# The state-space part of a two-layer block: steps of four tokens, two rounds in place of eight, and GpSimd's products moved to VectorE

## The chip, the cores and the metric

The kernel runs on one core of one Trainium2 chip. The metric is the device time of one execution in microseconds (us), from the core's first instruction to its last; it is reported as the median of several runs. The engines are named TensorE (PE, its weight loads PEld), VectorE (DVE), ScalarE (ACT), GpSimd (POOL) and SyncE (SP).

## The reference

`x` is 256 tokens by 1024 channels, float32. A first block of two layers (feed-forward, mixer, feed-forward; the mixers are attention with a gated linear recurrence, and a gated convolution) is followed by a second block of two layers, each a "mix2" mixer and a feed-forward part, the last one a mixture of 8 experts. Each mix2 mixer splits its input into a state-space group (S5, 512 channels) and a gated linear attention (GLA). Of the S5 group, cut to what matters (32 groups of 16 channels, 64 complex states each):

```python
lam_bar = jnp.exp(lam * dt)
b_bar = ((lam_bar - 1.0) / lam)[:, :, None] * b_mat
bu = jnp.einsum('gph,blgh->blgp', b_bar, u_c.astype(jnp.complex64))
a_cum, s = lax.associative_scan(_linear_recurrence_op, (a_elems, bu), axis=1)
states = s + a_cum * h[:, None]
y = jnp.einsum('ghp,blgp->blgh', c_mat, states).real
...
y = y.transpose(1, 0, 2, 3, 4).reshape(bsz, seq, S5_WIDTH) + d_skip.astype(f32) * uf
y = jax.nn.gelu(y).astype(u.dtype)
return y * jax.nn.sigmoid(y @ w_glu + b_glu)
```

The recurrence is s[t] = lam_bar * s[t-1] + bu[t], one complex number for each state.

## The kernel before

The program is a list of ten parts (`SUBS`, numbered b): 0 to 5 are the first block, 6 is mix2, 7 a feed-forward part, 8 mix2, 9 the experts. The second block's layer is n = (b - 6) // 2, so mix2 runs twice. A part eats "units" of weights: SyncE loads a unit (1 MB `raw_gu`, 0.5 MB `raw_d`) into one of two raw buffers, ScalarE rounds it (`hi`, into `wh_gu`, `wh_d`), VectorE takes the rest (`lo`, into `wl_gu`, `wl_d`), and TensorE multiplies in three terms (`mm3`). Each engine runs its own list in the order of the code; semaphores (`wait_ge`, `then_inc`) bind them, and `link` is a wait of an engine for its own last result.

In a feed-forward part (b = 5 and b = 7 here) TensorE does for each unit r the products of `gate_up(r)` (48 matmuls of 256 columns) and then `down(r-1)` (12 of 512 columns).

In mix2, TensorE first streams units U to U+5 (q, k, alpha, v, output gate `go`, and the S5 inputs u), and puts the eight level products of GLA (`level(j)`, L2047 and L2066) behind blocks of that stream; VectorE prepares each level (`differences`, `decayed`, `masked`), ScalarE does the exponentials (`decay`). Then comes the S5 stage. The states are turned by powers of the phase of lam_bar, so that the recurrence has a real factor and VectorE's scan instruction can do it: `table(n)` on GpSimd computes these powers `E` for all 256 tokens in feed-forward parts 5 and 7. Then eight rounds r follow, of two state tiles each: TensorE `bu(r)` (L2130), VectorE `turn_in(r)` (L1319 to L1322), a sum and a difference (L1339, L1340), four scans of 256 tokens (L1344), `turn_back(r)` (L1329, L1330), GpSimd two more products (L1705, L1706), TensorE the output products (L2154). `gated_heads` and `mixed_heads` of GLA lie in rounds 0 and 1; `skip(t)` adds the direct term. After them come gelu, XH and XL (L710, L1361), and TensorE's GLU unit, whose first matmul waits for `yl`. B and C of each round or layer come by DMAs that GpSimd issues.

## Time and profile before

| what | value |
|---|---|
| median of 3 runs | 2754.56 us (2746.49 to 2756.39) |
| span of the profiled execution | 2747.2 us |
| PE busy | 2600.3 us, 95% of the span |
| PEld busy | 2379.0 us, 87% |
| DVE busy | 2165.5 us, 79% |
| ACT busy | 1483.6 us, 54% |
| POOL busy | 947.8 us, 34% |
| mean granted TensorE clock | 0.971 |
| DMA | 670.58 MB, 244 GB/s on the mean |

The profile gives the profiled execution's own time as its span, 2747.2 us, which lies between the lowest and the highest of the three runs. Busy time is the sum of an engine's instructions; of TensorE it says how long it had matmuls in it, not that it ran at its peak. The granted clock is 1.0 at 2.4 GHz and 0.5 at 1.2 GHz. Times in the rows below are microseconds from the span's start; the first mix2 runs from about 1067 to 1243, the second from about 1497 to 1673.

### The profile page before, as it was taken

What the parts mean: (1) busy time and instruction counts of PE and PEld (TensorE: products, weight loads), DVE (VectorE), ACT (ScalarE), POOL (GpSimd) and SP (SyncE); (2) the same over time, 40 slices, a digit from 0 to 9 for tenths busy, and PEclk for the clock granted to TensorE, in tenths of its full rate; (3) what the DMA queues carried; (4) which work ended last, traced back from release to release, by engine and by line L of the source; (5) the groups of instructions that cost most, each with busy time, mean ns of one, the idle gap of its engine ahead of it and who ended that gap; (6) DMA issues with size and microseconds to landing.
All of it is one profiled execution on the core that took longest, in us unless ns stands there. A gap on an engine that the chain in (4) does not pass through costs nothing. (4 is left out here: it accounts for less than half of the span.)

```text
span 2747.2 us, 47482 instructions
## 1 busy us (share of the span) xinstructions
PE 2600.3 (95%) x17802; PEld 2379.0 (87%) x17802; DVE 2165.5 (79%) x2488; ACT 1483.6 (54%) x1930; POOL 947.8 (34%) x586
## 2 busy tenths in 40 slices
PE   8999899999998998888998978999999999999997
PEld 7999699999897998658998747999999999999986
DVE  5667666766787676987855997898989898989888
ACT  4337543443434334424334515777777777777765
POOL 6990089688789992126900130000000000000000
PEclk9999999999999998999999988999999999999999
DMA  8664267566566653324553415999999999999985
GB/s 309 252 237 148 103 241 256 202 250 254 191 241 229 220 183 134 115 105 164 183 184 138 164 63 192 343 350 333 352 335 349 338 347 343 347 345 346 340 320 216
DMA packets 129209, 670.58 MB, mean 244 GB/s; under 512 B 14672, under 2 KB 14992, under 8 KB 80064
## 3 DMA queue, kind: packets, MB, share of 16 engines
q1 hardware_dynamic: 111024, 604.72, 59.9%
q0 software_dynamic: 18064, 64.21, 6.9%
q8 instruction: 81, 1.33, 0.2%
q14 instruction: 40, 0.33, 0.0%
HBM read 667.82 MB, written 1.05 MB: 243 GB/s over the span
## 5 line engine op out<-in xcount | busy, mean ns | idle before, releaser
L1721 PE MATMUL work<-xT_hi,wh_gu 128*128 128x256 f32 x2088 | 593.9, 284 | 21.6 <-DVE xT_lo L985 12.0
L1722 PE MATMUL work<-xT_lo,wh_gu 128*128 128x256 f32 x2088 | 592.3, 284 | 0.0
L1723 PE MATMUL work<-xT_hi,wl_gu 128*128 128x256 f32 x2088 | 591.7, 283 | 0.0
L1721 PE MATMUL work<-wh_gu,mixT_hi 128*128 128x256 f32 x1792 | 507.5, 283 | 2.8 <-DVE wl_gu L1439 1.5
L1722 PE MATMUL work<-wl_gu,mixT_hi 128*128 128x256 f32 x1792 | 505.8, 282 | 0.0
L1723 PE MATMUL work<-wh_gu,mixT_lo 128*128 128x256 f32 x1792 | 505.5, 282 | 0.0
L857 DVE TENSOR_TENSOR wl_gu<-raw_gu,wh_gu 128x2048 fp32r<-128x2048 f32 x158 | 392.3, 2483 | 72.0 <-ACT wh_gu L395 71.5
L1721 PEld LDWEIGHTS work<-xT_hi,wh_gu 128*128 128x128 f32 x2088 | 401.3, 192 | 30.1 <-issue 21.3
L1722 PEld LDWEIGHTS work<-xT_lo,wh_gu 128*128 128x128 f32 x2088 | 401.7, 192 | 4.8
L1723 PEld LDWEIGHTS work<-xT_hi,wl_gu 128*128 128x128 f32 x2088 | 401.5, 192 | 0.0
L862 DVE TENSOR_TENSOR wl_d<-raw_d,wh_d 128x1024 fp32r<-128x1024 f32 x157 | 250.2, 1594 | 189.6 <-ACT wh_d L402 189.5
L1721 PE MATMUL acc<-wh_d,h_hi 128*128 128x512 f32 x912 | 380.4, 417 | 2.8 <-DVE wl_d L1444 2.7
L1723 PE MATMUL acc<-wh_d,h_lo 128*128 128x512 f32 x912 | 361.2, 396 | 0.0
L1722 PE MATMUL acc<-wl_d,h_hi 128*128 128x512 f32 x912 | 361.1, 396 | 0.0
L1721 PEld LDWEIGHTS work<-wh_gu,mixT_hi 128*128 128x128 f32 x1792 | 340.9, 190 | 12.5 <-DVE wl_gu L1439 1.7
L1722 PEld LDWEIGHTS work<-wl_gu,mixT_hi 128*128 128x128 f32 x1792 | 341.6, 191 | 8.8
L1723 PEld LDWEIGHTS work<-wh_gu,mixT_lo 128*128 128x128 f32 x1792 | 341.5, 191 | 0.0
L402 ACT ACTIVATE wh_d<-raw_d 128x1024 fp32r<-128x1024 f32 x157 | 166.2, 1059 | 276.1 <-PE acc L1723 276.1
L395 ACT ACTIVATE wh_gu<-raw_gu 128x2048 fp32r<-128x2048 f32 x158 | 300.7, 1903 | 25.4 <-PE acc L1723 25.0
L1652 POOL TENSOR_SCALAR scratch<-scratch,small 128x1024 f32<-128x1024 f32 x84 | 312.9, 3724 | 4.2
L1439 DVE TENSOR_TENSOR wl_gu<-raw_gu,wh_gu 128x2048 fp32r<-128x2048 f32 x113 | 259.1, 2293 | 38.0 <-ACT wh_gu L726 37.9
L1439 DVE TENSOR_TENSOR wl_gu<-scratch,wh_gu 128x2048 fp32r<-128x2048 f32 x112 | 256.6, 2291 | 25.5 <-ACT wh_gu L726 25.0
(436 smaller groups left out, 4785.6 us busy)
## 6 DMA issues: line engine op xcount, KB each, us to landing
raw_gu<-in_w_gu SPq DMA_DIRECT2D x271, 1024.0 KB, 5.2
raw_d<-in_w_d SPq DMA_DIRECT2D x269, 512.0 KB, 5.4
scratch<-in_w_gu SPq DMA_DIRECT2D x112, 1024.0 KB, 7.2
scratch<-in_w_d SPq DMA_DIRECT2D x112, 512.0 KB, 7.8
scratch<-in_w_mod POOLq DMA_DIRECT2D x96, 512.0 KB, 3.7
scratch<-in_s_b POOLq DMA_DIRECT2D x16, 256.0 KB, 2.9
rows<-in_norm_post POOLq DMA_DIRECT2D x6, 512.0 KB, 4.4
rows<-in_ln_g POOLq DMA_DIRECT2D x4, 512.0 KB, 5.5
```

The lines of the kernel that those rows point to most:

```text
L395: act.activation(wh_gu[k][:, :, :, :].rearrange("p a k n -> p (a k n)"), raw_gu[k][:, :], ACT.Copy).then_inc(gu_hi, 1)
L402: act.activation(wh_d[k][:, :], raw_d[k][:, :], ACT.Copy).then_inc(d_hi, 1)
L857: TT(wl, raw_gu[k][:, :], wh.bitcast(F32), ALU.subtract).then_inc(gu_lo, 1)
L862: TT(wl_d[k][:, :], raw_d[k][:, :], wh_d[k][:, :].bitcast(F32), ALU.subtract).then_inc(d_lo, 1)
L1439: TT(wl, RAW_GU[k] if k > 1 else RAW_GU[k][:, :], wh.bitcast(F32), ALU.subtract).then_inc(gu_lo, 1)
L1652: link(pool.tensor_scalar(MW[n % 3], MW[n % 3], c, None, ALU.mult))
L1721: pe.matmul(out_, w[0], m[0], start=start, stop=False)
L1722: pe.matmul(out_, w[0], m[1], start=False, stop=False)
L1723: return pe.matmul(out_, w[1], m[0], start=False, stop=stop)
```

## The change

The recurrence is taken four tokens at a time (`STEP` = 4). With lam4 = lam_bar to the fourth, the scan runs over 64 steps instead of 256, for a quarter of the columns. What a block of four tokens gives its last state is one product with stacked B matrices (`BF`, turned from `CW`), what the state before the block gives its four outputs is one product with stacked C matrices (`CW` afterwards), and what the inputs in a block give its own outputs, with the direct term, is one product with `LOCAL`. The inputs are laid out as `U4`: four tokens of 32 channels on 128 partitions, 64 columns.

What moves:
- **GpSimd**: `table(n)` makes 64 steps in place of 256, and is called in mix2 after the head gain's DMA, no longer in the feed-forward part before. In its old place stands `s5_matrices(n)`: 9 DMAs, C times the factor, three steps of powers of lam_bar on `CW` (18 tensor_tensor), and after TensorE's local product four steps more (24). Its two products of each round are gone.
- **TensorE**: `s5_products(n, r)` is put between `gate_up` and `down` of parts 5 and 7: 8 transposes, then 4 times 8 transposes, then 33 matmuls. The last units of the loops over units are written out. In mix2 there are two rounds: `bu(h)` 16 matmuls of 64 columns, `outputs(h)` 24 matmuls of 64 columns.
- **ScalarE**: `spread(h)` writes `U4` with 16 instructions of 32 partitions each half, `gathered_back(h)` does gelu in 16; `s5_evictions` copies what `s5_products` makes.
- **VectorE**: the C preparation (7 instructions at the start of mix2) goes; two rounds of `turn_in`, `scan` (2 and 16 short scans) and `turn_back` (6) replace the eight; `lo(U+6)` moves behind them.

The diff, cut to its core:

```diff
+STEP = 4
+TAIL, LEAD = 12, 10
...
+        PREPARED = [START[SECOND - 1], START[SECOND + 1]]
...
+                def spread(h, used, count):
+
+                    act.wait_ge(s["table"], n + 1)
                     act.wait_ge(used, count)
-                    act.activation(UT[:, t, :], PA[:, t % 2, 0:S], ACT.Copy).then_inc(g["u_sb"], 1)
+                    ps = PA[:, 2 * h:2 * h + 2, 0:S].rearrange("p t (c j) -> p t j c", j=STEP)
+                    to = U4.rearrange("p (t q) c -> p t q c", q=4)
+                    for q in range(4):
+                        for j in range(STEP):
+                            act.activation(to[32 * j:32 * j + 32, 2 * h:2 * h + 2, q, :], ps[32 * q:32 * q + 32, :, j, :],
+                                           ACT.Copy).then_inc(s["u4"], 1)
...
-                if b > SECOND:
-                    act.wait_ge(x_done, b)
...
+                act.wait_ge(x_done, b)
+                act.wait_ge(s["cw"], n + 1)
                 keep(4, AL, gu_used, U + 2)
...
+                def scan(h):
+                    x = PP[h]
+                    dve.wait_ge(s["bu_used"], 2 * n + h + 1)
+                    TT(x[0], x[0], x[1], ALU.add)
+                    link(TT(x[2], x[2], x[3], ALU.subtract))
+                    for w in (x[0], x[2]):
+                        for t in range(8):
+                            at = 16 * n + 8 * h + t
+                            last = dve.tensor_tensor_scan(w[:, t, :], s5p[:, 1, at:at + 1].broadcast_to([P, S // STEP]),
+                                                          w[:, t, :], 0.0, ALU.mult, ALU.add)
+                    last.then_inc(s["states"], 1)
...
+                dve.wait_ge(s["table"], n + 1)
                 turn_in(0)
...
+                scan(0)
+                dve.wait_ge(g["o"], n + 1)
+                turn_in(1)
+                gated_heads()
+                turn_back(0)
+                scan(1)
+                turn_back(1)
+                mixed_heads()
+                lo(U + 6)
+                lo(U + 7)
+                result_lo(0)
+                result_lo(1)
...
+                pool.wait_ge(s["c_ready"], n + 1)
+                pool.wait_ge(s["bt_sb"], 2 * (n + 1))
+                for j in range(STEP - 2, -1, -1):
+                    re0, im0 = (CW[:, c, :, j + 1, :] for c in range(2))
+                    re1, im1 = (CW[:, c, :, j, :] for c in range(2))
+                    TT(re1, re0, lr, ALU.mult)
+                    link(TT(u, im0, li, ALU.mult))
+                    link(TT(re1, re1, u, ALU.subtract))
+                    TT(im1, re0, li, ALU.mult)
+                    link(TT(u, im0, lr, ALU.mult))
+                    link(TT(im1, im1, u, ALU.add))
+                pool.memset(small[:, 6:7], 0.0).then_inc(s["powers"], 1)
...
-                    if b == 5:
+                    if b == SECOND - 1:
                         pool.wait_ge(par_ready, 1)
-                        table(0)
+                        s5_matrices(0)
...
                     pool.dma_start(wau[:, :], A["w_alpha"][n]).then_inc(alphaw_in, 16)
-                    pool.wait_ge(xt_l, 4 * (b + 1))
-                    pool.dma_start(CRAW, A["s5_c"][n]).then_inc(s5c_in, 16)
+                    table(n)
...
+            def s5_products(n, r):
...
+                if r == -11:
+                    pe.wait_ge(s5b_in, 128 * (n + 1))
+                    for c in range(2):
+                        for t in range(4):
+                            last = pe.transpose(PB[:, 2 + c, t * P:(t + 1) * P], BRAW[:, t, c, :], ident)
+                        last.then_inc(s["bt"], 1)
+                if -7 <= r <= -4:
+                    for k in (2 * r + 14, 2 * r + 15):
+                        c, st = turned_input(k)
+                        pe.wait_ge(s["powers"], n + 1)
...
+                if r == -3:
+                    pe.wait_ge(s["bf_sb"], 8 * n + 7)
+                    pe.wait_ge(s["c_ready"], n + 1)
+                    pe.matmul(PB[:, 2, :], ONTO, SKIP, start=True, stop=False)
+                    for st in range(16):
+                        for c in range(2):
+                            last = pe.matmul(PB[:, 2, 32 * st:32 * st + 32], stack(c, st), CP[:, c, st, :],
...
+                for r in range(nf - tail, nf):
+                    gate_up(n0 + r)
+                    s5_products(PREPARED.index(n0), r - nf + LEAD * PREPARED.index(n0))
+                    down(n0 + r - 1, 0, f0 + r - 1, 0, False, False)
...
-                            pe.wait_ge(g["u_sb"], 4 * n + t - 1)
-                        ps = PA[:, t % 2, 0:S]
+                            pe.wait_ge(g["gout"], n + 1)
+                        ps = PA[:, t, 0:S]
```

The first place is TensorE in feed-forward part 5, between a unit's `gate_up` (its last matmul, L1815) and the `down` that follows (L1813 into `acc`). Before, nothing stood between them. Now, for units 11, 15 and 19 of 22 (16 to 18 are like 15, and part 7 has the same at units 7, 11 to 14 and 15):

```order
L1815 MATMUL work<-xT_hi,wl_gu 128x256
L1912 MATMUL work<-const,scratch 128x128 [waits s5b_in]
L1912 MATMUL work<-const,scratch 128x128 x7
L1813 MATMUL acc<-wh_d,h_hi 128x512 [waits h_ready,d_lo]
...
L1815 MATMUL work<-xT_hi,wl_gu 128x256
L1921 MATMUL work<-const,scratch 128x128 [waits s5_powers]
L1921 MATMUL work<-const,scratch 128x128 x3
L1921 MATMUL work<-const,scratch 128x128 [waits s5_powers]
L1921 MATMUL work<-const,scratch 128x128 x3
L1813 MATMUL acc<-wh_d,h_hi 128x512 [waits h_ready,d_lo]
...
L1815 MATMUL work<-xT_hi,wl_gu 128x256
L1926 MATMUL work<-scratch 128x512 [waits s5_c_ready,s5_bf_sb]
L1929 MATMUL work<-scratch 128x32 x32
L1813 MATMUL acc<-wh_d,h_hi 128x512 [waits h_ready,d_lo]
```

So 8, then 8 in each of four units, then 33 instructions are now in the way of `down`, each group behind a wait for a DMA or for GpSimd.

The second place is VectorE in the S5 stage. Before, this is the end of round 0 and the start of round 1, one of eight:

```order
L1329 TENSOR_TENSOR rows<-scratch 128x512 [waits s5_states,gla_og]
L1330 TENSOR_TENSOR rows<-scratch 128x512
L1339 TENSOR_TENSOR scratch<-scratch 128x512 [waits s5_prod2,s5_prod,s5_bu_used]
L1340 TENSOR_TENSOR scratch<-scratch 128x512
L1344 SCALAR_TENSOR_TENSOR scratch<-s5p,scratch 128x256 [waits dve_step]
L1344 SCALAR_TENSOR_TENSOR scratch<-s5p,scratch 128x256 x3
L1319 TENSOR_TENSOR scratch<-acc,scratch 128x512 [waits s5_bu]
```

and now, round 0 of two, its sum, difference and 16 scans of 64 steps, and then the next `turn_in`; its `turn_back` of six instructions stands further on, behind `gated_heads`:

```order
L1372 TENSOR_TENSOR scratch<-scratch 128x512 [waits s5_bu_used]
L1373 TENSOR_TENSOR scratch<-scratch 128x512
L1377 SCALAR_TENSOR_TENSOR scratch<-s5p,scratch 128x64 [waits dve_step]
L1377 SCALAR_TENSOR_TENSOR scratch<-s5p,scratch 128x64 x15
L1364 TENSOR_TENSOR rows<-acc,scratch 128x512 [waits s5_bu,gla_o]
L1365 TENSOR_TENSOR rows<-acc,scratch 128x512
L1366 TENSOR_TENSOR rows<-acc,scratch 128x512
...
L1385 TENSOR_TENSOR scratch<-scratch 128x512 [waits s5_states,gla_og]
L1386 TENSOR_TENSOR scratch<-scratch 128x512
L1387 TENSOR_TENSOR scratch<-scratch 128x512
L1388 TENSOR_TENSOR scratch<-scratch 128x512
L1389 TENSOR_TENSOR scratch<-scratch 128x512 [waits dve_step]
L1390 TENSOR_TENSOR scratch<-scratch 128x512
```

The wait for GpSimd's products (`s5_prod2`) is gone, and the products with it are VectorE's.

The third place is ScalarE in mix2, from the last two exponentials of GLA. Before:

```order
L658 ACTIVATE scratch<-scratch 128x512 [waits gla_diff] x2
L654 ACTIVATE scratch<-acc 128x256 [waits gu_used]
L658 ACTIVATE scratch<-scratch 128x512 [waits gla_diff]
L688 ACT_TABLE_LOAD
L688 ACTIVATE const<-acc 128x1024 [waits gu_used]
L654 ACTIVATE scratch<-acc 128x256 [waits d_used]
L395 ACTIVATE wh_gu<-raw_gu 128x2048 [waits gu_used,gu_landed1]
L402 ACTIVATE wh_d<-raw_d 128x1024 [waits d_used,d_landed1]
L654 ACTIVATE scratch<-acc 128x256 [waits gu_used]
L654 ACTIVATE scratch<-acc 128x256 [waits d_used]
L395 ACTIVATE wh_gu<-raw_gu 128x2048 [waits gu_used,gu_landed0]
L698 ACTIVATE scratch,small<-work 128x128 [waits gla_o]
```

Now (L747 is the old L688, L755 the old L698):

```order
L718 ACTIVATE scratch<-scratch 128x512 [waits gla_diff] x3
L747 ACT_TABLE_LOAD
L747 ACTIVATE const<-acc 128x1024 [waits gu_used]
L701 ACTIVATE scratch<-acc 32x2x64 [waits d_used,s5_table]
L701 ACTIVATE scratch<-acc 32x2x64 x15
L701 ACTIVATE scratch<-acc 32x2x64 [waits d_used,s5_table]
L701 ACTIVATE scratch<-acc 32x2x64 x15
L407 ACTIVATE wh_gu<-raw_gu 128x2048 [waits gu_used,gu_landed1]
L414 ACTIVATE wh_d<-raw_d 128x1024 [waits d_used,d_landed1]
L755 ACTIVATE rows,small<-work 128x128 [waits gla_o]
```

Four instructions of 128 partitions have become 32 of 32 partitions, behind a wait for the table; on GpSimd the table's steps now stand between the two DMAs and the product (L1798, old L1688) for `gated_heads`:

```order
L1741 MEMSET small 128x1 [waits pool_step]
L1793 DMA rows<-in_head_gain 128x512 [waits x_done]
L1794 DMA w_alpha<-in_w_alpha 16x256
L1660 MEMSET scratch 128x16
L1661 MEMSET scratch 128x16
L1662 COPY s5p<-s5p 128x16
L1663 COPY s5p<-s5p 128x16
...
L1798 TENSOR_TENSOR const<-const,rows 128x1024 [waits headgain_in,gla_gout]
```

## Rows read from the trace of the kernel before

**Rows 1.** Windows: span, then busy us (instructions) of each engine, PEclk, DMA share, GB/s

```profile
1136.00:1212.00 76.00, 54.35 (x253) 32.98 (x249) 73.22 (x117) 12.71 (x26) 25.19 (x24) 0.89 0.17 58
...
1300.00:1350.00 50.00, 50.00 (x353) 46.80 (x353) 40.15 (x30) 18.75 (x18) 48.20 (x36) 1.00 0.52 181
...
1400.00:1450.00 50.00, 50.00 (x356) 47.02 (x355) 27.22 (x28) 19.10 (x17) 0.00 (x0) 1.00 0.52 187
```

**Rows 2.** Waits, 1075 to 1245: who waited for whom, total us, times, longest

```profile
DVE rows L1268 <- PE work L2047: 3.3, 2, 1.9
```

**Rows 3.** Timeline of VectorE: start us, us, engine, line, operation

```profile
1146.94 2.16 DVE L1298 SCALAR_TENSOR_TENSOR scratch<-work,small,const 128x128 f32<-128x128 f32 x8
...
1170.61 0.67 DVE L1319 TENSOR_TENSOR scratch<-acc,scratch 128x512 f32<-128x512 f32 x1
...
1175.85 2.44 DVE L1344 TENSOR_TENSOR_SCAN scratch<-s5p,scratch 128x256 f32<-128x256 f32 x4
1178.20 0.67 DVE L1319 TENSOR_TENSOR scratch<-acc,scratch 128x512 f32<-128x512 f32 x1
```

**Rows 4.** Timeline of TensorE around the S5 stage of the first mix2

```profile
1127.79 0.39 PE L1721 MATMUL acc<-xT_hi,wh_gu 128*128 128x256 f32 x1
...
1136.11 1.99 PE L2130 MATMUL acc<-scratch 128*128 128x256 f32 x8
...
1211.98 0.38 PE L1721 MATMUL work<-xT_hi,wh_gu 128*128 128x256 f32 x1 [1.06 <-DVE xT_lo L1361]
```

**Rows 5.** Timeline of TensorE: eight float32 matmuls (L1790), and around a transpose

```profile
1486.73 1.95 PE L1790 MATMUL work<-const,modT 128*128 128x128 f32 x16
1488.43 0.47 PE L1721 MATMUL acc<-wh_d,h_hi 128*128 128x512 f32 x1
...
1773.82 0.47 PE L1721 MATMUL acc<-wh_d,h_hi 128*128 128x512 f32 x1
1774.13 0.39 PE L1722 MATMUL acc<-wl_d,h_hi 128*128 128x512 f32 x1
```

**Rows 6.** Timeline of TensorE where its clock was low

```profile
1056.31 2.35 PE L1808 MATMUL work<-small,const 128*128 128x1 f32 x16
...
1059.52 0.63 PE L1723 MATMUL acc<-wh_d,h_lo 128*128 128x512 f32 x1
...
1166.68 4.47 PE L2154 MATMUL work<-rows,scratch 128*32 128x256 f32 x16 [3.41 <-DVE rows L1330]
1171.08 1.99 PE L2130 MATMUL acc<-scratch 128*128 128x256 f32 x8
```

**Rows 7.** Timeline of GpSimd: the table's start, a later step, DMAs of mix2

```profile
937.94 0.15 POOL L1604 MEMSET scratch<- 128x16 f32 x1
...
980.02 2.14 POOL L1625 TENSOR_TENSOR s5p<-s5p 128x16 f32<-128x16 f32 x1
...
1007.40 1.04 POOL L1617 TENSOR_TENSOR scratch<-scratch,s5p 128x512 f32<-128x512 f32 x1
...
1017.36 1.04 POOL L1617 TENSOR_TENSOR scratch<-scratch,s5p 128x512 f32<-128x512 f32 x1
...
1515.53 0.59 POOL L1682 DMA_DIRECT2D rows<-in_head_gain  x1 [144.17 <-DVE residual L1009]
```

**Rows 8.** Timeline of ScalarE: units 11, 15 of part 5, mix2's gate, small copies

```profile
964.90 0.39 ACT L523 ACTIVATE scratch<-work 128x256 f32<-128x256 f32 x1 [2.81 <-PE work L1723]
...
999.03 0.39 ACT L523 ACTIVATE scratch<-work 128x256 f32<-128x256 f32 x1 [2.82 <-PE work L1723]
...
1129.50 1.03 ACT L688 ACTIVATE const<-acc 128x1024 f32<-128x1024 f32 x1
...
1559.65 1.03 ACT L688 ACTIVATE const<-acc 128x1024 f32<-128x1024 f32 x1
...
1701.31 0.27 ACT L758 ACTIVATE scratch<-work 128x128 f32<-128x128 f32 x1
1701.47 0.28 ACT L764 ACTIVATE h_hi<-acc 128x128 fp32r<-128x128 f32 x1
```

More of the change, by code:

```diff
@@ L221, in program @@
         most_members = s5i[0:1, NE:NE + 1]
-        LATE_Y, LATE_T = JUNK, view(3072, S)
+        LATE_Y, LATE_T = view(7168, 1024), view(3072, S)
+        SGM = [view(4096 + 256 * i, 256) for i in range(2)]
+        HFM = [view(4608 + 256 * i, 256) for i in range(2)]
         cols_in, consts_in, router_in = (sem(n) for n in ("cols_in", "consts_in", "router_in"))
@@ L228, in program @@
             sem(n) for n in ("gain_in", "lruw_in", "ln_in", "headgain_in", "alphaw_in"))
-        s5b_in, s5c_in = [sem(f"s5b_in{i}") for i in range(2)], sem("s5c_in")
+        s5b_in, s5c_in = sem("s5b_in"), sem("s5c_in")
         gu_landed = [sem(f"gu_landed{i}") for i in range(2)]
@@ L1079, in ffn @@
                     first, steps, reg = 1, chain.n, chain.reg
-                with dve.Fori(0, nf // 2 - first) as j:
+                tail = TAIL + LEAD * PREPARED.index(n0) if n0 in PREPARED else 0
+                looped = (nf - tail) // 2 - first
+                with dve.Fori(0, looped) as j:
                     chain.n, chain.reg = steps, reg + j * 4
@@ L1083, in ffn @@
                         step(r, j * 2)
-                chain.n, chain.reg = steps + 4 * (nf // 2 - first), reg
+                chain.n, chain.reg = steps + 4 * looped, reg
+                for r in range(nf - tail, nf):
+                    step(r, 0)
             mixed = [0]
@@ L1203, in mix2 @@
                 lo(U + 2)
[L1205 to L1214 removed]
+                dve.wait_ge(s["cw"], n + 1)
                 dve.wait_ge(g["z"], n + 1)
@@ L1357, in mix2, with table_half, turn_in @@
[L1357 to L1361 removed]
+                def table_half(h):
+                    return E[:, 0, 8 * h:8 * h + 8, :], E[:, 1, 8 * h:8 * h + 8, :]
+                def turn_in(h):
+                    er, ei = table_half(h)
+                    vr, vi = (s5_input(h, c).rearrange("p (t c) -> p t c", t=8) for c in range(2))
+                    x = PP[h]
+                    dve.wait_ge(s["bu"], 2 * n + h + 1)
+                    TT(x[0], vr, er, ALU.mult)
+                    TT(x[1], vi, ei, ALU.mult)
+                    TT(x[2], vi, er, ALU.mult)
+                    TT(x[3], vr, ei, ALU.mult).then_inc(s["bu_used"], 1)
@@ new lines, in turn_back @@
+                def turn_back(h):
+                    er, ei = table_half(h)
+                    x = PP[h]
+                    dve.wait_ge(s["states"], 2 * n + h + 1)
+                    TT(x[1], x[0], er, ALU.mult)
+                    TT(x[4], x[2], ei, ALU.mult)
+                    TT(x[3], x[2], er, ALU.mult)
+                    link(TT(x[5], x[0], ei, ALU.mult))
+                    TT(x[1], x[1], x[4], ALU.subtract)
+                    TT(x[3], x[3], x[5], ALU.add).then_inc(s["hr"], 1)
@@ L1630, in table @@
-                pool.memset(small[:, 6:7], 0.0).then_inc(s["table"], 1)
+                while w < S // STEP:
+                    pr, pi = (pw[:, c].unsqueeze(2).broadcast_to([P, 16, w]) for c in range(2))
+                    et = ET[:, 0:16 * w].rearrange("p (t s) -> p t s", t=16)
+                    re0, im0 = E[:, 0, :, 0:w], E[:, 1, :, 0:w]
+                    re1, im1 = E[:, 0, :, w:2 * w], E[:, 1, :, w:2 * w]
+                    TT(re1, re0, pr, ALU.mult)
+                    link(TT(et, im0, pi, ALU.mult))
+                    link(TT(re1, re1, et, ALU.subtract))
+                    TT(im1, re0, pi, ALU.mult)
+                    link(TT(et, im0, pr, ALU.mult))
+                    link(TT(im1, im1, et, ALU.add))
+                    w *= 2
+                    if w < S // STEP:
+                        squared()
@@ L1713, in _ @@
                 if b == SECOND + 1:
-                    table(1)
+                    s5_matrices(1)
         @block.tensor
```

376 lines of the change are left out of this document (188 added, 188 removed).

## The prediction

> **What bounds the kernel now.** I first read the stages. In the first mix2's S5 stage VectorE is busy 73.22 us of 76 and TensorE waits in it, at a granted clock of 0.89 [rows 1]: VectorE sets the pace. In the feed-forward part TensorE is busy 50.00 of 50 us, with GpSimd at work beside it (48.20) or not (0.00) [rows 1]: there every instruction added to TensorE lengthens the time, and GpSimd's and VectorE's are free. The stage before S5, GLA's levels, is set by TensorE's stream, but closely: VectorE waited there only 3.3 us for level products [rows 2]. So the change takes work from where VectorE bounds, and puts some where TensorE bounds.
>
> The S5 stage runs from `bu(0)` at 1136.1 to the GLU's first matmul at 1212.0 [rows 4]: 75.9 us. A steady round costs VectorE 7.6 us (1170.61 to 1178.20), in which one 512-column instruction takes 0.6 and a scan of 256 steps 0.59 (2.35 for four) [rows 3]. The second mix2 repeats it.
>
> **The change, on the clock of before.** I follow the first mix2 and leave out what is inserted earlier.
>
> *Start of the stage.* `u_[2]` started at 1127.8 [rows 4]; now it waits for the gate's eviction, over at 1130.5 [rows 8]: 2.7 us. `table` now runs on GpSimd beside GLA. Beside GpSimd's table VectorE was busy 40.15 us in 50, without it 27.22 [rows 1]; that is up to 0.26 us for each us of GpSimd's work (unit phases differ, so it is rough; I take 0.22). Over the 28 us of levels: 6 us, less the 3.3 it waited [rows 2], and a little for the exponentials: 4. So `bu(0)` starts at 1142.8. The C preparation that goes lies where VectorE then waits for TensorE's alpha product; I count 0. `spread` is 32 small ScalarE instructions. Two of 128 columns follow each other by 0.16 us [rows 8]; strided they may take 0.3. Then 2.6 to 4.8 us a half, beside TensorE's `u_[3]` and level 7: hidden; if it weren't, at most 5.
>
> *The rounds.* `bu(0)`: 16 matmuls. Eight float32 matmuls took 1.70 us (1486.73 to 1488.43) [rows 5], 0.21 each; fewer columns don't help (the 1-column ones of [rows 6] are no quicker: 16 records, eight matmuls, 2.35). So 3.4, to 1146.2. Then VectorE: `turn_in` 2.4; sum and difference 1.4 with a wait for its own result; 16 scans of 64 steps. No row shows such a scan: a quarter of 0.59 is 0.15, no saving is 0.59; with a fixed part I take 0.2, 3.2 in all. `turn_in(1)` 2.4, `gated_heads` 2.4 (2.16 and a reciprocal [rows 3]), `turn_back(0)` six instructions 3.8, `scan(1)` 4.6, `turn_back(1)` 3.8. Together 24.0: 1170.2. The removed GpSimd products leave no wait. `outputs(1)`: 24 matmuls, 5.1; `row_of(6)` and `row_of(7)`, 12 matmuls of 512 columns each, 5.6 at full clock (gap 0.23, about what 1773.82 to 1774.13 shows with a transpose ahead [rows 5]). Gelu in 16 pieces and the XL part (4.5) lie beside these 5.6. TensorE idles about 10 us before `outputs(0)`; after a wait of 3.41 us it worked 4.4 us at half clock [rows 6], so I add 1.5. GLU starts at 1182.4: **29.6 us sooner**. `lo(U+6)` and the loads behind it come later, but land before ScalarE is free for them; if not, up to 3 us.
>
> *Second mix2.* `table(1)` can't start before the head gain's DMA, 1515.5 [rows 7], which needs VectorE's residual. In part 5 its first 42.1 us (937.94 to 980.02) [rows 7] hold all six levels the short table needs; two more squarings and the busier VectorE make about 50. It ends at 1566.5, when the gate has been out since 1560.7 [rows 8], 1564.7 with the 4 us above. So `spread` is late by 2 and its first half no longer hidden: 3 us less, **26.6**.
>
> *What feed-forward parts pay.* 40 transposes: one between matmuls of 512 columns lengthened 0.23 to 0.31, and it filled a pipeline gap; 0.08 to 0.21 each, I take 0.11, 4.4 us. 33 local products, 0.21 each and the 512-column one 0.6 more: 7.6. Six switches 0.1 each. 12.6 us, in each layer: **25.2**. Next the clock. At 1056.31 to 1058.5 eight 1-column matmuls ended at half clock with no wait before, and a 512-column one then lasted 0.63 for 0.39 [rows 5, 6]. The local products have 32 columns, between these and the 128 of L1790, that left the clock alone. If it falls, 6 us; half of that, 3, for each layer: **6**.
>
> *GpSimd's race.* ScalarE copies the first transposes about 5.8 us after unit 11's gate (964.9): 0.9 of transposes, 2.8 of `down` (12 matmuls by 0.23), 1.0 for its half of the weights, which comes first in its list, and 1.1 for two copies: 970.7. The powers are three groups of six 512-column instructions. Such a group took 10.0 us (1007.40 to 1017.36) [rows 7], up to 11; three are 31. Ready: 1001.8. TensorE asks after unit 15's gate, 999.0 plus 0.9 inserted: 999.9 [rows 8]. Late by **2** us, in part 7 the same (also four units): **4**. The four groups after the local product (41 us) end about 1075; mix2 asks for them only at its fifth eviction, some 20 us after its start at 1067.
>
> Sum: −29.6 −26.6 +25.2 +6 +4 = −21. The profiled execution spans 2747.2 us, inside the runs' 2746.5 to 2756.4 and 0.3% under their median; I predict against the span, 2747 − 21 = 2726.
>
> **A page against these rows.** The Trainium skill, SBUF — State Buffer, "Who interferes with whom", says a VectorE instruction with two SBUF inputs contends with a GpSimd one that reads SBUF, the later one blocked until the other ends. By this rule each table instruction could hold up a GLA instruction, which is the first rival; the 12.9 us between the windows of [rows 1] agree in kind.
>
> **The rivals.**
> - *Contention beside GLA.* Each of GpSimd's table instructions holds up one of VectorE's: then not 0.22 but up to 0.5 us for each us of table, 14 over the levels, 25 over the whole. For it: levels leave VectorE 3 us. Against: [rows 1] show half of that. Bound at zero: 4 us better each. Price: 10 us more in each layer: 2746, no change. 0.17.
> - *Clock.* Matmuls of 32 and 64 columns keep TensorE at half clock: `outputs(1)` and the two row blocks 9 us longer, local 3 more: 24 for both layers less some cover, 2745. For it: [rows 6], 1 column. Against: `bu` follows dense work. 0.13.
> - *The powers come late (the other side).* If a GpSimd instruction on the strided views of `CW` takes 2.0 us more than its 1.7, the group of 18 is 36 late, twice: 2726 + 72 = 2798. It decides from 0.95 more on each (17 us late a layer, 2760). Against: `table` wrote strided views too. 0.06.
> - *Cheap preparation, short scans.* Transposes at 0.08, no clock loss, scans 0.15, GLA unhurt: 8 to 10 less per layer, 2707. 0.12.
> - *It doesn't do what it says*: VectorE's stage isn't shortened. Nothing speaks for it. 0.02.
>
> **The numbers.** The forecast itself has 0.50, and its own range is 2713 to 2740 (each layer's start ±4, scans and transposes ±3). For 8 in 10 the range reaches to the cheap case and over both rivals at no change: 2704 to 2754. What a measurement tells from no change is 0.5%, 13.7 us: faster means under 2733.5. The forecast gives 0.40, the cheap case 0.12, the first rivals 0.06: 0.58. Slower (above 2761): late powers 0.05, tails 0.04: 0.09. The same: 0.33.
>
> **What would show it.** From `bu(0)` to GLU's first matmul 40 us where it was 76; VectorE's scans at 0.2; a unit's period in part 5 at 8.5 except where `s5_products` stands; TensorE's wait for `powers` near 2 us; no GLA wait for VectorE longer than 4. It is wrong if TensorE stands in mix2 before `bu(0)` for `u4`, if `powers` are 10 late, if the row of L1322 (old L1268) grows, or if the clock of the feed-forward parts falls after the local products.

## The result, and the profile after

The changed kernel takes 2762.9 us (median of 7 runs, 2760.1 to 2764.1), the kernel before on the same chip 2748.0: ratio 1.0048, 95% interval 1.0037 to 1.0058. Measured again beside the last experiments it was 1.0059 (1.0043 to 1.0075). I had forecast 2726, in a range of 2704 to 2754: wrong, and on the other side.

Its profiled execution spans 2761.8 us, 14.6 more than the one before. Three lines of the diff's functions help in reading: in the changed file the gates of part 5 are copied out of PSUM in L534 (before: L523), the S5 outputs are L2264 and L2267, the GLU's and all weight products are L1813 to L1815. Windows of the first layer, with the columns of [rows 1] (the last three lie inside the others):

```profile
990.00:1041.00 51.00, 47.81 (x333) 44.62 (x332) 27.19 (x25) 20.01 (x24) 10.89 (x8) 0.97 0.43 155
1041.00:1052.00 11.00, 11.00 (x68) 10.66 (x67) 1.28 (x4) 0.11 (x1) 0.62 (x1) 0.71 0.25 96
1052.00:1087.00 35.00, 34.52 (x191) 30.45 (x190) 20.22 (x18) 15.75 (x26) 32.92 (x25) 0.80 0.30 106
1097.00:1168.00 71.00, 64.59 (x452) 56.44 (x452) 48.17 (x68) 34.69 (x52) 35.10 (x60) 0.93 0.30 111
1168.00:1187.00 19.00, 12.07 (x100) 11.47 (x96) 16.22 (x43) 15.64 (x38) 0.00 (x0) 0.87 0.01 2
1187.00:1216.00 29.00, 28.52 (x120) 26.55 (x120) 17.45 (x33) 14.80 (x36) 1.14 (x2) 0.56 0.38 145
...
1041.00:1045.00 4.00, 4.00 (x36) 3.76 (x34) 1.28 (x4) 0.11 (x1) 0.00 (x0) 1.00 0.57 213
1046.00:1051.00 5.00, 5.00 (x25) 5.00 (x25) 0.00 (x0) 0.00 (x0) 0.00 (x0) 0.50 0.00 0
1183.00:1187.00 4.00, 1.97 (x8) 1.57 (x8) 3.93 (x8) 2.01 (x3) 0.00 (x0) 0.50 0.00 0
```

Read the PEclk column. The S5 stage (1168 to 1216) is 48.2 us in place of 75.9, so the change does what it says: VectorE is no longer the bound. But in its last 29 us TensorE is busy 28.52 and has a clock of 0.56: it is the bound now, at nearly half speed. The local products (second row) have 0.71; the two windows of a feed-forward part in [rows 1] had 1.00. They start at full clock and fall to half on the way: 36 records in 4 us at 1.00, then 25 in 5 us at 0.50, so a float32 matmul of 32 columns takes 0.22 us first and about 0.4 after the fall. The last row shows that the clock had already fallen ahead of `outputs(0)`, while TensorE was busy 1.97 us of 4.

The timeline of TensorE has the same story instruction by instruction (a float32 matmul leaves two records, a transpose one):

```profile
1001.32 1.97 PE L1921 MATMUL work<-const,scratch 128*128 128x128 f32 x8 [3.19 <-POOL small L1728]
...
1041.39 9.91 PE L1929 MATMUL work<-scratch 128*128 128x32 f32 x64
1051.11 0.77 PE L1813 MATMUL acc<-wh_d,h_hi 128*128 128x512 f32 x1
1051.69 0.63 PE L1814 MATMUL acc<-wl_d,h_hi 128*128 128x512 f32 x1
...
1096.87 0.55 PE L1813 MATMUL work<-xT_hi,wh_gu 128*128 128x256 f32 x1 [4.02 <-DVE xT_lo L1043]
...
1132.79 0.72 PE L2195 MATMUL work<-scratch 64*128 64x128 f32 x8 [3.60 <-DVE scratch L1304]
...
1158.36 0.55 PE L1813 MATMUL acc<-xT_hi,wh_gu 128*128 128x256 f32 x1 [2.81 <-ACT const L747]
...
1168.07 3.79 PE L2253 MATMUL acc<-scratch 128*128 128x64 f32 x32
...
1183.56 1.97 PE L2243 MATMUL work<-const 128*128 128x128 f32 x8 [5.46 <-DVE const L1346]
...
1187.42 0.69 PE L2264 MATMUL work<-scratch 128*128 128x64 f32 x2 [1.89 <-DVE scratch L1390]
1187.91 1.06 PE L2267 MATMUL work<-scratch 128*128 128x63 f32 x4
...
1207.93 0.77 PE L1813 MATMUL acc<-wh_gu,mixT_hi 128*128 128x512 f32 x1
...
1216.25 0.39 PE L1813 MATMUL work<-xT_hi,wh_gu 128*128 128x256 f32 x1 [0.30 <-DVE xT_lo L1395]
```

ScalarE's gates beside it, of part 5's units 15, 16, 19 and 20; by [rows 8] a unit took 8.53 us:

```profile
998.16 0.38 ACT L534 ACTIVATE scratch<-work 128x256 f32<-128x256 f32 x1 [2.81 <-PE work L1815]
...
1012.51 0.38 ACT L534 ACTIVATE scratch<-work 128x256 f32<-128x256 f32 x1 [1.86 <-PE work L1815]
...
1040.73 0.38 ACT L534 ACTIVATE scratch<-work 128x256 f32<-128x256 f32 x1 [1.85 <-PE work L1815]
...
1062.07 0.39 ACT L534 ACTIVATE scratch<-work 128x256 f32<-128x256 f32 x1
```

TensorE has a wait for the powers (3.19), one for VectorE in GLA (3.60), one for the gate (2.81), and two for VectorE ahead of the outputs (5.46 and 1.89). `bu(0)` at 1168.07 and the GLU at 1216.25 answer to [rows 4]. The two outputs, 48 matmuls, fill 1187.4 to 1207.9. VectorE's and ScalarE's rows (first the levels of GLA, then the S5 stage):

```profile
1127.61 1.51 DVE L1297 TENSOR_TENSOR scratch<-scratch 128x256 f32<-128x256 f32 x1
...
1131.24 1.49 DVE L1304 TENSOR_TENSOR scratch<-scratch 128x256 f32<-128x256 f32 x1
...
1133.66 0.41 DVE L1304 TENSOR_TENSOR scratch<-scratch 128x256 f32<-128x256 f32 x1
...
1175.80 3.02 DVE L1377 TENSOR_TENSOR_SCAN scratch<-s5p,scratch 128x64 f32<-128x64 f32 x16
...
1194.81 0.69 DVE L1390 TENSOR_TENSOR rows<-rows 128x512 f32<-128x512 f32 x1
1197.96 6.67 ACT L711 ACTIVATE scratch<-work 32x128 f32<-32x128 f32 x16 [10.49 <-PE work L2267]
1208.20 6.61 ACT L711 ACTIVATE scratch<-work 32x128 f32<-32x128 f32 x16 [2.91 <-PE work L2267]
```

GpSimd's signals: the powers ready (L1728), and the table ready in the first and the second mix2 (L1681):

```profile
1001.16 0.10 POOL L1728 MEMSET small<- 128x1 f32 x1
...
1132.51 0.10 POOL L1681 MEMSET small<- 128x1 f32 x1
...
1588.32 0.10 POOL L1681 MEMSET small<- 128x1 f32 x1
```

Waits from 880 to 1960, both layers (who for whom, total us, times, longest):

```profile
DVE rows L1322 <- PE work L2176: 21.4, 6, 6.9
...
PE acc L1813 <- ACT const L747: 5.7, 2, 2.9
...
PE work L2176 <- DVE scratch L1304: 4.2, 1, 4.2
PE work L2195 <- DVE scratch L1304: 3.6, 1, 3.6
```

The same VectorE instruction (L1304, one level of GLA and the next) takes 1.49 us while GpSimd's last table level runs, and 0.41 once the table has ended (1132.51).

**A table of stages.** Single times of one kernel spread over 10 us and more on a chip, but these stages repeat within 0.6 us (in the two traces of each of the two kernels). So I compare stages. GLA is the least steady: versions that leave it alone lie between 69.5 and 72.8. All are differences of two starts on TensorE: *GLA* from the stream's first product (behind its wait for `xT_lo`) to `bu(0)`; *S5* from `bu(0)` to the GLU's first product; *part 7* from its first product (1253.40 in the trace above) to the second stream's; *end* from the second GLU to the span's end. In us (my differences of rows):

| kernel | GLA 1, 2 | S5 1, 2 | part 7 | end | span |
|---|---|---|---|---|---|
| before | 61.9, 61.9 | 75.9, 75.9 | 255.2 | 1105.1 | 2747.2 |
| before_again | 62.5, 62.0 | 76.0, 75.8 | 255.5 | 1105.2 | 2747.9 |
| changed | 71.2, 72.8 | 48.2, 48.2 | 278.0 | 1109.4 | 2761.8 |
| after_again | 71.3, 72.5 | 48.2, 48.2 | 278.0 | 1109.2 | 2763.1 |
| bt_early | 72.8, 72.6 | 48.2, 48.1 | 271.5 | 1109.6 | 2746.9 |
| no_local | 70.0, 71.2 | 48.2, 48.2 | 266.8 | 1109.9 | 2742.5 |
| keep_busy | 71.1, 71.9 | 41.2, 41.1 | 277.9 | 1108.5 | 2748.8 |
| table_hole | 67.1, 66.9 | 48.2, 48.2 | 278.0 | 1109.8 | 2761.2 |
| local_spread | 69.5, 72.7 | 48.2, 48.2 | 274.6 | 1109.5 | 2753.9 |
| level6_first | 70.0, 71.3 | 48.2, 48.2 | 277.7 | 1107.9 | 2754.7 |
| gather_split | 71.4, 72.4 | 46.9, 46.6 | 277.8 | 1104.8 | 2753.4 |
| all_six | 63.0, 64.2 | 43.6, 40.7 | 270.0 | 1109.7 | 2720.5 |
| best | 64.0, 63.9 | 40.7, 40.7 | 268.1 | 1105.0 | 2709.7 |

### The profile page after: what moved, and what is told of

Same layout as the page of the kernel before. It is cut to its first block, busy times and chain, and to the rows that moved or that the text cites. A ratio compares the mean times of both kernels' runs of the same rounds, so it can differ in the third digit from the quotient of the medians.

```text
span 2761.8 us, 47491 instructions
## 1 busy us (share of the span) xinstructions
PE 2623.6 (95%) x17950; PEld 2435.9 (88%) x17950; DVE 2092.8 (76%) x2391; ACT 1542.0 (56%) x2098; POOL 934.3 (34%) x606
## 4 chain that ended last, share of the span: by engine, by line
PE 84%; DVE 9%; ACT 3%; POOL 2%; issue 1%; DMA 0%; SPq 0%; DVEq 0%; ACTq 0%; POOLq 0%
PE work L1813 16%; PE work L1814 16%; PE work L1815 16%; PE acc L1813 9%; PE acc L1814 9%; PE acc L1815 9%; DVE wl_gu L911 1%; PE work L2332 1%; PE work L2267 1%; PE acc L2392 1%; DVE wl_d L916 1%; PE work L1900 1%; PE work L1871 1%; PE work L1929 1%; DVE mixT_lo L1155 1%
## 5 line engine op out<-in xcount | busy, mean ns | idle before, releaser
L1813 PE MATMUL work<-xT_hi,wh_gu 128*128 128x256 f32 x2088 | 595.2, 285 | 22.7 <-DVE xT_lo L1043 12.3
L1815 PE MATMUL work<-xT_hi,wl_gu 128*128 128x256 f32 x2088 | 592.7, 284 | 0.0
L1813 PE MATMUL work<-wh_gu,mixT_hi 128*128 128x256 f32 x1792 | 508.0, 283 | 2.9 <-DVE wl_gu L1488 1.5
L1815 PE MATMUL work<-wh_gu,mixT_lo 128*128 128x256 f32 x1792 | 505.8, 282 | 0.0
L1813 PEld LDWEIGHTS work<-xT_hi,wh_gu 128*128 128x128 f32 x2088 | 402.4, 193 | 32.0 <-issue 22.1
L1815 PEld LDWEIGHTS work<-xT_hi,wl_gu 128*128 128x128 f32 x2088 | 402.7, 193 | 0.0
L916 DVE TENSOR_TENSOR wl_d<-raw_d,wh_d 128x1024 fp32r<-128x1024 f32 x157 | 241.6, 1539 | 211.5 <-ACT wh_d L414 211.3
L1813 PE MATMUL acc<-wh_d,h_hi 128*128 128x512 f32 x912 | 383.4, 420 | 2.7 <-DVE wl_d L1493 2.7
L1815 PE MATMUL acc<-wh_d,h_lo 128*128 128x512 f32 x912 | 362.9, 398 | 0.0
L1813 PEld LDWEIGHTS work<-wh_gu,mixT_hi 128*128 128x128 f32 x1792 | 341.4, 190 | 12.6 <-DVE wl_gu L1488 1.7
L1815 PEld LDWEIGHTS work<-wh_gu,mixT_lo 128*128 128x128 f32 x1792 | 341.8, 191 | 0.0
L1763 POOL TENSOR_SCALAR scratch<-scratch,small 128x1024 f32<-128x1024 f32 x84 | 279.1, 3322 | 4.2
```

The source lines that it names most:

```text
L916: TT(wl_d[k][:, :], raw_d[k][:, :], wh_d[k][:, :].bitcast(F32), ALU.subtract).then_inc(d_lo, 1)
L1763: link(pool.tensor_scalar(MW[n % 3], MW[n % 3], c, None, ALU.mult))
L1813: pe.matmul(out_, w[0], m[0], start=start, stop=False)
L1815: return pe.matmul(out_, w[1], m[0], start=False, stop=stop)
```

## The experiments

The theory: what I missed is TensorE's clock (pauses and stretches of narrow matmuls, and what stands behind them) and GpSimd's table beside GLA. The rival: the added instructions themselves cost more than I had priced.

**The powers in time.** In both lists, PE's and ScalarE's:

```
-                if r == -11:
+                if r == -12:
```

> The B transposes and their two evictions stand one unit earlier (r == -12), so GpSimd starts the powers sooner; nothing else moves. In the changed kernel's trace TensorE waited 3.18 us for the powers in each feed-forward part, and that unit took 14.35 us: 8.53, eight transposes 0.87, the wait 3.18, and 1.8 more in which transposes and products ran at half clock. Clock theory: the wait goes and the 1.8 behind it too, 4.9 us in each part, 9.9 in all: about 2753. Wait alone (the 1.8 belong to the transposes themselves): 3.2 in each part, 6.4 in all: about 2756.5, with this unit at about 11.2 us.

2753.4 us, ratio 1.0009 (0.9999 to 1.0019). ScalarE's gates, and the window around them:

```profile
988.27 0.39 ACT L534 ACTIVATE scratch<-work 128x256 f32<-128x256 f32 x1 [2.81 <-PE work L1815]
996.80 0.39 ACT L534 ACTIVATE scratch<-work 128x256 f32<-128x256 f32 x1 [2.82 <-PE work L1815]
1006.21 0.39 ACT L534 ACTIVATE scratch<-work 128x256 f32<-128x256 f32 x1 [1.85 <-PE work L1815]
```

```profile
985.00:1025.00 40.00, 40.00 (x293) 37.86 (x293) 23.35 (x22) 16.35 (x19) 6.27 (x4) 1.00 0.50 171
```

The unit with the first two transposed groups takes 9.41 us (996.80 to 1006.21), 8.53 plus 0.88: of the 5.82 that it took more, 3.2 were the wait and 1.8 the clock behind it. That is the clock theory. Part 7 is 6.5 shorter, not 4.9: the unit with the local products took 19.7 in place of 21.3, since the clock fell later in them. These 1.6 us are not the edit's: in the first layer table_hole, level6_first and gather_split, which leave this code alone, have 19.7 or 19.8 too, while keep_busy and both traces of the changed kernel have 21.3. When the clock falls in that stretch differs from trace to trace; the wait and what stood behind it are 4.9 in each part.

**The local products.** Without them, with wider ones, and spread. no_local leaves out the loop over `st` and keeps the one 512-column matmul ahead of it. wide_local reads 128 columns with the same weights; besides the number of columns it changes what is read, and each matmul starts its own sum:

```
                     for st in range(16):
                         for c in range(2):
-                            last = pe.matmul(PB[:, 2, 32 * st:32 * st + 32], stack(c, st), CP[:, c, st, :],
-                                             start=False, stop=st == 15 and c == 1)
+                            last = pe.matmul(PB[:, 2, P * (st % 4):P * (st % 4) + P], stack(c, st), stack(c, st),
+                                             start=True, stop=True)
```

> Left out: the 32 matmuls of 32 columns of the local products, in both layers; the 512-column one ahead of them stays, and the evictions read what stands in the bank, so the state-space part's own-token term is garbage. Price of instructions alone (my prediction's 0.21 each): 6.7 us a layer, 13.4 in all: 2749.5. Clock theory: the 9.9 us that they took go, and with them the half clock of the eight products behind them (0.43 for 0.23 us each, with the next ones 2.2) and, in the first layer, the 1.9 us that the modulation's columns took more than before: 14.0 and 12.1, together 26: about 2737.

2743.3 us, ratio 0.9962 (0.9944 to 0.9980): by the two ratios 0.9% under the changed kernel, some 24 us (19 between the traces), where the price of instructions gave 13. From unit 11's gate to the stream part 5 is 12.0 shorter and part 7 is 11.2; I had 14.0 and 12.1 by the clock, 6.7 by the price.

> The 32 local matmuls of each layer keep their weights but read 128 columns in place of 32 (columns of the stacked matrices, each starting its own sum); so the own-token term is garbage and more columns are computed. If few columns cost the clock: 128 columns take about 0.23 us each at full clock, 7.4 us for 32, the products behind them stay at 0.23 us, and the unit with the local products takes 17 us, where it took 21.3: 4 to 6 us less a layer, about 2753. If it is the number of matmuls or of weight loads, whatever their columns: the clock falls as before, each takes 0.31 us or more, and the time is 2763 or longer.

Its garbage reached the router too, and the experts' part took five times as long (7145 us in all, ratio 2.596, 2.591 to 2.601); only the rows ahead of it are read. TensorE at the first layer's local products, and the windows over them:

```profile
1045.36 7.31 PE L1929 MATMUL work<-scratch 128*128 128x128 f32 x64
...
1052.43 0.48 PE L1813 MATMUL acc<-wh_d,h_hi 128*128 128x512 f32 x1
1052.74 0.40 PE L1814 MATMUL acc<-wl_d,h_hi 128*128 128x512 f32 x1
```

```profile
1045.00:1052.00 7.00, 7.00 (x62) 6.76 (x61) 1.26 (x4) 0.09 (x1) 0.00 (x0) 1.00 0.45 152
```

32 matmuls of 128 columns took 7.1 us (1045.36 to 1052.43) at a clock of 1.00; 32 of 32 columns had taken 9.7 (1041.39 to 1051.11) at 0.71. Four times the columns, 2.6 us less, and the products behind them lasted 0.40, not 0.63. The engine had not paused in either. Part 7 was 4.5 shorter. So it is the narrowness that costs here, through the clock, and not the number of matmuls: as long as the clock is full, the narrow ones take 0.22 us each, as the wide ones do. That each wide one starts its own sum is not tested apart.

Spread: the 16 tiles' pairs are put in a list, and each group of three products takes one from it.

```
                 pe.matmul(out_, w[0], m[1], start=False, stop=False)
-                return pe.matmul(out_, w[1], m[0], start=False, stop=stop)
+                last = pe.matmul(out_, w[1], m[0], start=False, stop=stop)
+                if between:
+                    between.pop(0)()
+                return last
```

> The 32 local matmuls of 32 columns stand no longer in one block of 9.9 us but two at a time behind each three products of the unit (256 or 512 columns); their number and work are the same. Clock theory: it is the stretch of nothing but narrow matmuls that lowers the clock; spread, they take 0.21 us each at full clock, 6.7 us, and nothing behind them is slow: 5.6 us less in each layer and the 1.9 of the modulation's columns in the first: 13, about 2750. Rival: a narrow matmul costs 0.31 us wherever it stands, or switching back and forth costs as much: the unit stays at about 21 us and the time at 2763.

2758.2 us, ratio 1.0021 (1.0006 to 1.0036).

```profile
1040.00:1045.00 5.00, 5.00 (x47) 1.00 0.44 125
1045.00:1050.00 5.00, 5.00 (x46) 1.00 0.49 193
1050.00:1055.00 5.00, 5.00 (x33) 1.00 0.00 0
```

(PE alone, clock, DMA share, GB/s.) The clock stays at 1.00, but part 7 is only 3.4 shorter, not 5.6. The switching is not why. The two units that hold the narrow matmuls took 26.8 us, 9.7 more than two of 8.53; in this 9.7 are the last transposed group (0.88), a wait of 0.63 for ScalarE, and about 0.9 for the 512-column matmul, which leaves 7.3 us, 0.23 for each of the 32. In the gate's products three wide ones take 0.36 us alone and 0.80 with two narrow ones behind them, 0.22 for each. The missing 2.2 us are that wait, 1.0 in the unit behind them, where TensorE waits 0.75 for the low parts of its weights, and 0.22 or 0.23 where I had 0.21. So the clock theory holds: spread, the narrow matmuls keep their price at full clock.

**The outputs.** Around them TensorE multiplies something nobody reads:

```
+                def keep_busy(count):
+                    for _ in range(count):
+                        pe.matmul(PB[:, 3, :], XH[:, 4, 0:P], XH[:, 4:6, :].rearrange("p k s -> p (k s)"),
+                                  start=True, stop=True)
                 bu(1)
+                keep_busy(20)
                 heads_transposed()
+                keep_busy(8)
                 outputs(0)
+                keep_busy(12)
                 outputs(1)
```

> Added in each mix2: idle matmuls of 512 columns into a bank that nobody reads, 20 behind bu(1), 8 behind the head transposes, 12 between the two outputs, where TensorE waits for VectorE (5.5, 1.9 and about 3 us). Nothing else changes. Clock theory: TensorE reaches outputs(0) at full clock, and its 24 matmuls take 5.2 us, not 10.2; outputs(1) the same; the GLU then starts about 7 us sooner in each layer: 14 in all, about 2749. Rival one: matmuls of 64 columns pull the clock down themselves; outputs(0) starts fast and ends slow, 2 to 4 us gained a layer, about 2757. Rival two: 0.43 us is their price at any clock, and nothing changes: 2763.

2747.5 us, ratio 0.9987 (0.9975 to 1.0000).

```profile
1170.00:1189.00 19.00, 17.25 (x124) 15.41 (x123) 16.39 (x44) 15.61 (x37) 0.00 (x0) 1.00 0.01 2
1189.00:1202.00 13.00, 13.00 (x104) 12.42 (x104) 12.90 (x29) 6.99 (x17) 0.00 (x0) 1.00 0.05 8
1202.00:1211.00 9.00, 6.42 (x32) 5.12 (x31) 4.21 (x4) 7.88 (x18) 1.14 (x2) 0.99 0.95 365
```

```profile
1189.93 0.61 PE L2267 MATMUL work<-scratch 128*128 128x63 f32 x4
...
1210.79 0.58 PE L1813 MATMUL work<-xT_hi,wh_gu 128*128 128x256 f32 x1 [2.58 <-DVE xT_lo L1395]
```

Four records take 0.61 us, where they took 1.06; the stage is 41.2 and 41.1 us in place of 48.2: the 7 us of the clock theory, out of matmuls whose results nobody uses. The 48 matmuls of 64 columns run at full clock to their end, so here it was the pauses ahead of them that cost the clock, and not their 64 columns. The 2.58 in the last row says what is late next: the gather, which the slow clock had covered.

**The table.** GpSimd builds it while it waits for the local products.

```
                 pool.memset(small[:, 6:7], 0.0).then_inc(s["powers"], 1)
+                table(n)
                 pool.wait_ge(s["local"], n + 1)
...
-                    table(n)
                     pool.wait_ge(g["gout"], n + 1)
```

> GpSimd builds the table of E in the feed-forward part, in the 50 us in which it waits for the local products, and no longer beside GLA; the last preparation step takes its temporary from other places, nothing else changes. Contention theory: in the changed kernel's mix2 VectorE's 256-element instructions took 1.07 to 1.51 us beside the last table level (410 to 430 ns otherwise), so that TensorE waited 3.60 us and then 4.20 us in the second layer, and ran the next products at half clock. With no table beside them none is over 0.5 us, the time from the stream's first product to bu(0) is 66 us in each layer (61.9 of the kernel before, the gate's wait of 2.8 and its half clock of 1.5), where it was 71.2 and 72.8: 12 us less, about 2751. Rival: VectorE was late for its own queue (the weights' low parts, the wait for cw), and TensorE still waits 3 us or more there: about 2763. Second rival: the table now holds up VectorE in the feed-forward part: then the units with GpSimd at work take over 8.53 us.

2760.4 us, ratio 1.0029 (1.0016 to 1.0041). VectorE at the place of the two slow rows above:

```profile
1134.32 0.42 DVE L1299 TENSOR_TENSOR scratch<-scratch 128x256 f32<-128x256 f32 x1
...
1136.86 0.41 DVE L1306 TENSOR_TENSOR scratch<-scratch 128x256 f32<-128x256 f32 x1
```

No such instruction is over 0.43, TensorE's waits of 3.60 and 4.20 are gone, GLA takes 67.1 and 66.9 us (4.1 and 5.9 less), and part 7 is unchanged at 278.0. Part 5 is no longer than in the changed kernel, so the second rival fails too. The whole time shows little of these 10 us: in the trace the first stream starts 9.0 us later than in the changed kernel's, for part 5 itself starts 10.6 us later, and nothing ahead of it was changed.

**Level 6 first.** `level(6)` stands ahead of `stream(U + 5, ...)` and no longer behind `u_[2]` in it.

> In both mix2, TensorE does level 6 of GLA (1.16 us) ahead of u_[2] in place of behind it, where it waits for the gate's eviction. If TensorE's wait of 2.8 us is filled by it: 1.2 us less a layer, 2.3 in all; with a shorter pause the half clock behind it (1.5 and 2.1 us) may go too, then up to 6. Rival: level 6 itself waits for VectorE's masks or exponentials as long: no change.

2758.4 us, ratio 1.0028 (1.0013 to 1.0042). TensorE's wait for the gate is 1.25 and 0.34 us, from 2.81 and 2.90. GLA is 1.2 and 1.4 us shorter, which lies inside its spread between versions; only the waits show the effect.

**The gather alone.**

```
+                    act.activation(WHOLE[h], s5_output(h), ACT.Gelu_apprx_tanh).then_inc(s["whole"], 1)
...
-                                           ACT.Gelu_apprx_tanh).then_inc(s["gelu"], 1)
+                                           ACT.Copy).then_inc(s["gelu"], 1)
```

One gelu for the whole half, then eight small copies on ScalarE and eight on VectorE.

> Alone, the split gather (one gelu of 512 columns, then eight copies on ScalarE and eight on VectorE): behind outputs(1) TensorE has the two row blocks to do, 8.0 and 6.7 us at half clock in the two layers, and the old gather ended 0.30 and 1.56 us after them. If TensorE's row blocks now bound, the S5 stage gets 0.3 and 1.6 us shorter, 2 us in all, no difference in the time. If the gather was the bound by itself, 3 us a layer.

2758.3 us, ratio 1.0034 (1.0019 to 1.0048). S5 is 1.3 and 1.6 shorter, where the waits had been 0.30 and 1.56: TensorE's row blocks bound it. In the first layer 1.0 more came from them, which took 7.0 us in place of 8.0; the edit does not touch them.

**A second trace of each.**

> The kernel before once more, for a second trace of it. Open so far: of the changed kernel's 14.6 us, 4.3 lie behind the second GLU, in code that the change leaves alone (the router's 64 records took 138 ns each before and 222 after). If that is the clock's chance, a second trace of the kernel before may show 1105 to 1110 us from the second GLU's first matmul to the end, where the first had 1105.1 and the changed versions 1107.9 to 1109.9. If it belongs to the change, this trace shows 1105 again. Its two S5 stages should be 75.9 us again.

2749.9 us (one run). The end is 1105.2 again.

> The changed kernel once more, beside the versions of it on the same chip: its stages again within 1 us of 71.2, 48.2, 278.0, 72.8 and 48.2 us, and 0.3 to 0.6% over the kernel before. If the time ahead of part 5's eleventh unit differs by several us from the first trace's, that part is chance, and whole times of single runs can't be compared to better than that.

2765.1 us, ratio 1.0059 (1.0043 to 1.0075). The long end does not go with the change as such: gather_split and best, which have it and leave that code alone like all the others, have 1104.8 and 1105.0, as the kernel before, while the other versions have 1107.9 to 1109.9. In the first pair of traces the router's 16 matmuls of 8 columns hold 2.6 of the 4.3 us: 4.4 us before and 7.0 after, part of it at full clock before and all at half clock after. What decides which end a version gets I have not tested.

**All together.**

> Six edits together: B transposes a unit earlier, local products spread, the table in the feed-forward part, level 6 ahead of u_[2], idle matmuls around the outputs, and the gather of the result split: one gelu of 512 columns, then eight small copies on ScalarE and eight on VectorE, where ScalarE did 16 small gelus of 417 ns. If the clock and the contention are the whole of what the prediction missed, the savings add: 9.9, 13, 12, 2, 15, and for the gather what TensorE waited for it with the idle matmuls (2.6) and the half clock behind (1.5), 4 a layer: 8. Together 60: about 2703, 1.6% under the kernel before. If savings hide one another (one wait behind the other), 2720 to 2735. If one of them was chance of the clock, more.

2720.5 us, ratio 0.9878 (0.9851 to 0.9905). The single savings had been added up to 60 us; between the traces it is 41, so they hide one another in part.

> The six edits together with two small corrections: 11 idle matmuls in place of 8 ahead of outputs(0), and the first local product two groups of products later, so that it does not wait for ScalarE (0.63 us a layer). In the trace of the six edits the first layer's S5 stage took 43.6 us with outputs(0) falling to half clock in its middle, the second's 40.7. If the fall comes from the 0.9 us pause ahead of outputs(0), both are now 40.7, and with the waits gone the time is 2715 to 2718; if it was chance, 2716 to 2722. Both are about 1.2% under the kernel before.

2718.2 us, ratio 0.9894 (0.9872 to 0.9916), 1.1% under the kernel before. Its trace is the shortest of all, but its ratio and that of all_six can't be told apart.

```profile
1154.00:1195.00 41.00, 37.85 (x268) 33.88 (x264) 37.30 (x91) 26.30 (x60) 1.16 (x2) 1.00 0.22 77
```

Both S5 stages take 40.7 us at a clock of 1.00; in all_six the first had 43.6, with outputs(0) at half clock from its middle on. That the shorter pause ahead of it (0.23 us for 0.92) is why is not shown, and the traces speak against it: the same 0.92 stands in both layers of keep_busy and in the second of all_six, and the clock stayed full there. What made it fall in the midst of matmuls of 64 columns is open, and they may have a part in it. Against after_again's span (53.4 less) the stages give GLA 7.2 and 8.6, S5 7.5 and 7.5, part 7 9.9, the end 4.3 and all ahead of the first stream 8.3.

## Why the prediction was wrong, by its own steps

**Right.** The bound of before, and VectorE's rounds: from `bu(0)` to the last `turn_back` 27.4 us (1168.07 to 1195.50), and I had 3.4 + 24.0. Scans of 64 steps took 0.19 each. The transposes: five batches of eight, 0.87 to 0.88 each, 4.4 in a layer. `spread` is 4.65 a half and hidden. The gate's wait was 2.81 for 2.7. The powers were ready at 1001.2, forecast 1001.8, but this is luck in part: the trace ran 1.7 us ahead of the old one, so the powers were 1.1 late against unit 11's gate, and TensorE's wait for them was 3.19, not 2.

**The step that failed** is the price of TensorE's clock: the sum had 1.5 us for the outputs in each mix2, 3 for the local products in each layer, and nothing behind the waits. In three places the runs show more:
- *Outputs and row blocks.* I had 5.1 and 5.6, and 1.5 for the clock. Together 12.2; between VectorE's last row and the GLU lie 20.8 us: outputs(0) still ran till 1197.7, outputs(1) took 10.2, the row blocks 8.0. The rival "clock of 32/64-column matmuls" foresaw this slow stretch; I gave it 0.13. `bu` argued against it and does run at full clock, with 64 columns too, but behind dense work. The outputs follow two pauses (5.46 and 1.89 us), and the clock was at half before the first of them started: the pauses took it, and not the few columns. I had counted about 10 us of idling and priced it by one row of [rows 6]. keep_busy: 7.0 us a layer.
- *Local products.* 7.6 and 3 forecast, 13.1 measured in both layers (in the first the unit of 21.34 from 1040.73 to 1062.07 and the next of 8.85, less twice 8.53), and 1.9 more in the first layer, where the modulation's columns took 7.6 us for 5.7 at the low clock.
- *Behind every wait.* I priced waits at their length. Behind the powers stood 1.8 us of half clock. Behind the gate the 24 products took 4.5 and 5.1 us for 3.1, behind VectorE the 12 took 4.5 for 3.0.

**Contention beside GLA** was in the sum at 4 us a layer, and table_hole shows 4.1 and 5.9. So this term held, 1.9 short in the second layer; the first rival, which put 10 on top of it, did not come true. That the size came out is luck in part. I had spread 0.22 us over all levels and let 3.3 us of slack absorb some of it; it fell into one chain, the last table level beside `differences` and `decayed`, and a mean over 50 us can't show that.

With the rule of the Trainium skill, SBUF — State Buffer, "Who interferes with whom", which the prediction set beside this rival, the traces agree: 1.49 us beside GpSimd's reads, 0.41 without.

Of my signs three spoke against the forecast: the clock fell in the local products and stayed low behind them, TensorE waited 4.20 us for VectorE in the second GLA, and the row of L1322 (L1268 in [rows 2], 3.3 us in one layer) grew to 21.4 us over both. Its two longest waits, 6.3 and 6.9 us, are for the level that stands behind TensorE's wait for the gate.

**Hidden, then not.** I put the gather beside the row blocks. It takes 6.6 us, not 4.5 with all that follows, and was just late: 0.30 and 1.56. At the full clock that I had forecast it would have been later, by the 2.58 of keep_busy.

**Forecast, then nothing.** The second mix2 was to lose 3 us more, `spread` being late behind the table. The table took 44.6 us (1543.7 to 1588.3), not 50, and was ready ahead of the gate's end at 1593.8; `bu(0)` waited for nothing.

The sum: forecast −21. The first mix2 gained 18.4 for 29.6, the second 16.8 for 26.6, part 5 cost 24.4 for 17.6 (unit 11's gate to the stream), part 7 22.8. Misses of 11.2, 9.8, 6.8 and 5.2, the end's 4.3, less 1.7 that the trace was ahead of the old one before part 5: 35.6, and −21 + 35.6 = 14.6. Of the 11.2 and 9.8, the S5 stages hold 8.6 each. Part 7's 5.2 lie at the powers (3.2 and 1.8 for 2) and at the local products (13.1 for 10.6); part 5 has the modulation's columns on top. The 4.3 of the end and the 1.7 belong to no step of the prediction.

## What to carry to other kernels

When work moves from VectorE to TensorE, price TensorE's new instructions at both clocks, and ask what the engine did just before them: here pauses of 2 to 6 us, and a stretch of 32-column matmuls, left it and the wide ones behind it at half clock for some us. If TensorE will wait anyway, fill the wait, with real work moved there (level 6; moving the row blocks was not tried) or with idle matmuls. GpSimd's table belongs where VectorE has slack in its longest chain, which a mean over a window does not show.
